# Padded pitches for the stationary operands, and a first input projection issued term by term

## What is computed

```python
def reference(...):
    x = first_block(x, ...)    # rmsnorm, w_in (2048x4096), Fourier mixing and dilated attention,
                               # w_out, rmsnorm, w_up (2048x8192), relu^2, w_down, rmsnorm
    return second_block(x, ...)  # modulated rmsnorm, w_in_2, gated linear attention and convolution,
                                 # w_out_2, SwiGLU with 5632 hidden columns, rmsnorm
```

```python
proj = jnp.einsum('bsd,de->bse', u, w_in[layer])     # the first input projection
...
a = jnp.square(jax.nn.relu(jnp.einsum('bsd,df->bsf', u, w_up[layer])))
h = h + jnp.einsum('bsf,fd->bsd', a, w_down[layer])
...
x_next = x_next + gt2 * ((silu(h2 @ w_ffn_gate) * (h2 @ w_ffn_up)) @ w_ffn_down)
```

## Time and profile before

| | us |
|---|---|
| median of 3 runs | 2323.5 (2321.68 to 2323.79) |
| the profiled execution, its own time | 2323.11 |
| its span, first to last instruction | 2321.4 |
| mean granted TensorE clock | 0.996 of full speed |

### The profile page before, as it was taken

How to read it: one execution, slowest core, us unless ns; L and a number is a source line. 1 busy time by engine, 2 the same in 40 slices (tenths; PEclk the granted TensorE clock), 3 DMA queues, 4 the chain that set the end, 5 groups by cost and what they waited for, 6 DMA issues and landing times.

```text
span 2321.4 us, 29200 instructions
## 1 busy us (share of the span) xinstructions
PE 2281.5 (98%) x10465; PEld 1878.2 (81%) x10465; DVE 1539.1 (66%) x1822; ACT 1108.7 (48%) x1515; POOL 146.2 (6%) x213
## 2 busy tenths in 40 slices
PE   8999999999999999999999999998999999999997
PEld 6888888888878888888878877787888888888886
DVE  7987658868867877886767665556545544555545
ACT  5445455545544545545563463544444344444444
POOL 1110001101111111110001000000000000000000
PEclk9999999999999999999999999999999999999999
DMA  9884459888887898886677663564555655555553
GB/s 342 294 277 154 146 180 319 305 277 289 280 290 248 270 304 263 276 278 214 219 239 249 210 202 127 196 211 156 189 192 184 216 188 193 188 193 195 186 181 109
DMA packets 245188, 523.92 MB, mean 226 GB/s; under 512 B 20016, under 2 KB 20288, under 8 KB 243776
## 3 DMA queue, kind: packets, MB, share of 16 engines
q1 hardware_dynamic: 213680, 404.80, 53.4%
q0 software_dynamic: 29568, 111.97, 13.9%
q10 hardware_dynamic: 1808, 5.37, 0.6%
HBM read 517.87 MB, written 4.21 MB: 225 GB/s over the span
## 4 chain that ended last, share of the span: by engine, by line
PE 94%; DVE 3%; issue 1%; ACT 1%; DMA 0%; ACTq 0%; DVEq 0%; POOLq 0%
PE acc L1595 29%; PE acc L1597 29%; PE acc L1596 29%; PE tp L1610 2%; DVE wlo L957 1%; PE m L1621 1%; DVE macc L977 1%; PE tp L1919 0%; ACT whi L493 0%; PE tp L1937 0%; PE tp L1931 0%; PE tp L1844 0%; PE m L1729 0%; PE tp L1905 0%; DMA mring<-w_mod 0%
## 5 line engine op out<-in xcount | busy, mean ns | idle before, releaser
L493 ACT ACTIVATE whi<-wring 128x1024 fp32r<-128x1024 f32 x776 | 812.8, 1051 | 1067.7 <-PE acc L1597 1064.5
L957 DVE TENSOR_TENSOR wlo<-wring,whi 128x1024 fp32r<-128x1024 f32 x776 | 932.6, 1213 | 581.6 <-ACT whi L493 577.7
L1595 PE MATMUL acc<-whi,xhi 128*128 128x512 f32 x2112 | 831.8, 394 | 1.8 <-DVE wlo L957 1.6
L1597 PE MATMUL acc<-whi,xlo 128*128 128x512 f32 x2112 | 822.8, 390 | 0.0
L1596 PE MATMUL acc<-wlo,xhi 128*128 128x512 f32 x2112 | 822.3, 389 | 0.0
L1595 PEld LDWEIGHTS acc<-whi,xhi 128*128 128x128 f32 x2112 | 396.8, 188 | 92.8 <-issue 11.8
L1597 PEld LDWEIGHTS acc<-whi,xlo 128*128 128x128 f32 x2112 | 396.6, 188 | 83.4
L1596 PEld LDWEIGHTS acc<-wlo,xhi 128*128 128x128 f32 x2112 | 396.9, 188 | 80.8 <-issue 0.7
L977 DVE SCALAR_TENSOR_TENSOR macc<-mring,csil,macc 128x512 f32<-128x512 f32 x480 | 344.2, 747 | 36.3 <-DMA mring<-w_mod 30.1
L1597 PE MATMUL acc<-whi,alo 128*128 128x512 f32 x608 | 238.0, 391 | 3.6 <-issue 3.6
L1595 PE MATMUL acc<-whi,ahi 128*128 128x512 f32 x608 | 240.1, 395 | 1.3 <-DVE wlo L957 1.2
(11 more groups left out here) (226 smaller groups left out, 1050.4 us busy)
## 6 DMA issues: line engine op xcount, KB each, us to landing
wring<-w_up SPq DMA_DIRECT2D x216, 512.0 KB, 4.6
wring<-w_down SPq DMA_DIRECT2D x216, 512.0 KB, 5.0
mring<-w_mod POOLq DMA_DIRECT2D x192, 512.0 KB, 5.2
wring<-w_in SPq DMA_DIRECT2D x184, 512.0 KB, 5.5
wring<-w_gate SPq DMA_DIRECT2D x88, 512.0 KB, 4.4
wring<-w_out SPq DMA_DIRECT2D x64, 512.0 KB, 4.8
gbig<-ctx_in POOLq DMA_DIRECT2D x2, 1024.0 KB, 9.3
hspill<-h ACTq DMA_DIRECT2D x1, 2048.0 KB, 7.9
```

The source lines that it names most:

```text
L493: act.activation(whi[:, piece_slot(c, piece), 0:half], wring[:, g4, piece * half:(piece + 1) * half], ACT.Copy).then_inc(hi_done, 1)
L957: dve.tensor_tensor(wlo[:, h4, 0:half], wring[:, g4, piece * half:(piece + 1) * half], whi[:, h4, 0:half].bitcast(F32), ALU.subtract).then ...
L1595: pe.matmul(dst, hi[:, tile, rows], whi[:, h4, w], start=(kg == first and k == 0), stop=False)
L1597: last = pe.matmul(dst, lo[:, tile, rows], whi[:, h4, w], start=False, stop=(kg == final and k == KG - 1))
```

## The change

Three things are changed. `xhi` and `xlo` are declared with 260 values for each k tile, of which 256 are used: a pitch of 1040 bytes. `ahi` and `alo` get 258 (1032 bytes), `bhi` and `blo` 257 (1028 bytes). To make room, `vrows` shares its place with `blk`, which is written later; an unused tensor `fill` keeps `gbig` on the place of `ctx_place`. The second change is in `multiply`: with `by_term=True` the 6 matmuls of a k tile are issued as hi·whi for t = 0 and 1, hi·wlo for t = 0 and 1, lo·whi for t = 0 and 1. This is used in blocks 1 to 7 of the first input projection. Each PSUM bank receives the same three products in the same order.

```diff
-        xhi = sb("xhi", [P, KT, S], F32R)
-        xlo = sb("xlo", [P, KT, S], F32R)
+        xhi = sb("xhi", [P, KT, S + 4], F32R)[:, :, 0:S]
+        xlo = sb("xlo", [P, KT, S + 4], F32R)[:, :, 0:S]
...
-        vrows = sb("vrows", [P, 3, P])
...
+        with ExitStack() as ph:
+            vrows = sb("vrows", [P, 3, P], scope=ph)
         blk = sb("blk", [P, T, NB])
...
-            ahi = sb("ahi", [P, KT, S], F32R, scope=ph)
-            alo = sb("alo", [P, KT, S], F32R, scope=ph)
+            ahi = sb("ahi", [P, KT, S + 2], F32R, scope=ph)[:, :, 0:S]
+            alo = sb("alo", [P, KT, S + 2], F32R, scope=ph)[:, :, 0:S]
...
+            sb("fill", [P, 4 * KT], scope=ph)
             gbig = sb("gbig", [P, 2 * D], scope=ph)
...
-            bhi = sb("bhi", [P, KT, S], F32R, scope=ph)
-            blo = sb("blo", [P, KT, S], F32R, scope=ph)
+            bhi = sb("bhi", [P, KT, S + 1], F32R, scope=ph)[:, :, 0:S]
+            blo = sb("blo", [P, KT, S + 1], F32R, scope=ph)[:, :, 0:S]
...
-            def multiply(hi, lo, kgs, kgroups, pair, order=None, operand=None):
+            def multiply(hi, lo, kgs, kgroups, pair, order=None, operand=None, by_term=False):
...
-                            for t in range(T):
+                            for term, (x, w_part) in enumerate(((hi, whi), (hi, wlo), (lo, whi)) if by_term else ()):
+                                for t in range(T):
+                                    last = pe.matmul(acc[:, 2 * pair + t, :], x[:, tile, t * P:(t + 1) * P], w_part[:, h4, w],
+                                                     start=(kg == first and k == 0 and term == 0),
+                                                     stop=(kg == final and k == KG - 1 and term == 2))
+                            for t in range(0 if by_term else T):
...
-                    multiply(xhi, xlo, range(3), 4, n % 2)
+                    multiply(xhi, xlo, range(3), 4, n % 2, by_term=True)
                     if n % 2 == 0:
                         reduce_mod(32, True)
-                    multiply(xhi, xlo, (3,), 4, n % 2)
+                    multiply(xhi, xlo, (3,), 4, n % 2, by_term=True)
```

## The result

The changed kernel takes 2362.8 us (median of 3 runs, 2362.67 to 2362.84) against 2323.5 us before: a ratio of 1.0173, with a 95% interval of 1.0154 to 1.0191. That is 39.3 us more, outside the range of 2262 to 2346 us, on the side that had the smallest chance. The profiled execution took 2362.7 us, with a span of 2361.0 us, 39.6 more than before.

What follows compares the result with a forecast made beforehand. The prediction took TensorE's rate of 226.7 ns per matmul as the bound. Its terms summed 0 + 0 + 0 against the profiled 2323.1 us and the median of 2323.5, giving 2323.3 us, with a range of 2262 to 2346.

Steps and rivals of the forecast that it cites:

- What bounds the kernel: Whole kernel: TensorE's rate, 9216 matmuls at 226.7 ns, 2089 of 2321.4 us; one nanosecond of the rate is 9.2 us.
- Part 1, can it quicken the stream: Pitches of the stationary operands in `multiply`: no quicker stream, taken as 0, with −99 us as the end.
- The second reading: Projections, w_up and w_ffn_down: distances 0, 512, 256 and 768 modulo 1024 bytes all have 226.7 ns; counted against a gain.
- Part 1, can it slow the loads: Weight loads in `multiply`: misaligned starts stay hidden behind the stream, taken as 0; other end 23 us more.
- rival C: Loads starting off 16 bytes need more than 226.7 ns and TensorE waits: 2346 to 2380 us; chance 0.14.
- A: Rival: the matmul stream quickens through starts finer than 128 bytes; at most −99 us, 2224, half of it 2274; chance 0.2.
- the bound of 99 us: Largest gain in `multiply`: all 9216 matmuls at the 216 ns of plain float32, 10.7 ns less each.
- The writes: Some 150 ScalarE and VectorE instructions writing rows with a small hole: 0 per instruction; `vrows` and `fill` also 0.
- Part 2, term by term: New order of 672 matmuls in the first projection's blocks 1 to 7: 0, with ends −7.2 and +2.2 us.
- Rival B: Gap in w_up and lower clock after idling are spared, together 7.0 us, giving 2316; chance 0.07 with the term order's −7.2.

## Why the prediction was wrong

**What bounds the kernel** was right. TensorE is the path in both, the producers stayed behind their cover, and one nanosecond of the rate was worth what the prediction said: the 5 to 6 ns found in the settled rows are the 39 us.

**Part 1, can it quicken the stream:** no gain was right, but the reason given is the step that failed, for it also ruled out a loss. The prediction took 113.3 ns for 256 columns with a load of 32 and 226.7 for 512 with a load of 128 for one law, 17/16 of the columns, and concluded that the loss goes with the columns streamed and so can't depend on the stationary's place. Two things differed between those rows, the columns and the load, and two points can't tell them apart. With full loads 256 columns take 120.0 ns. The loss is about the same for each matmul, 13.3 to 15 ns with a full load, and 6.7 ns in `multiply_rank`. That this part belongs to a meeting of load and stream is argued and not shown. What is shown is that the place of the stationary operand changes the rate: 226.7 ns at distance 0, 228.9 to 234.3 at nearly all others, for the worse and never for the better. The term that the prediction put at 0 was 39 us.

**The second reading was blind.** Distances of 0, 256, 512 and 768 with one rate were taken as evidence that the distance doesn't matter. All four are the same modulo 256. In `multiply_rank` the distance does change, between 0 and 128 modulo 256 from one k tile to the next (a weight slice there has 128 bytes), and the rate stays; but its loads have 32 columns. The prediction saw part of this ("no row shows a distance that isn't" a multiple of 128) and gave the unseen side a chance of 0.2 for a gain, but for a loss only by another mechanism.

**Part 1, can it slow the loads:** rival C had the sign and nearly the time, 2346 to 2380, by the wrong mechanism. The loads didn't grow: the group of x still means 188 ns, as the page of after has it.

```profile
L1602 PEld LDWEIGHTS acc<-whi,xhi 128*128 128x128 f32 x1888 | 355.1, 188 | 89.5 <-issue 9.8
```

And starts off 16 bytes were not the condition: x, whose starts all are multiples of 16, has 30 of the 47 us in the sum above. C priced 1704 matmuls at 13.3 ns; in fact nearly all 9216 lost something, 5 to 6 ns in the mean of a stage. The bound of the cost was therefore set by one candidate's mechanism (a longer load hidden behind 226.7 ns), and not by the nearest row of a disturbed stream, which the prediction had in hand and used for part 2 only: 230 ns after transposes. That 3.3 ns on 9216 matmuls is 30 us, 2354; with it the range would have reached most of the way. Its own test half worked: "Part 1 is wrong if the distance differs between x, a and b, in the order of 16, 8 and 4 bytes". The distance from start to start does differ, but in another order (231.6, 233.3, 232.6), which fits neither A nor C. Two smaller slips change nothing here: the range begins at 2262 although A's half, which it was to end with, is 2274, and the bound of 99 us takes 256 columns of plain float32 for 512 steps of the array, which no row shows.

The Trainium skill, in "TensorE: Matmul & The Clock Gate", section "Part 2: What happens when you issue a matmul", was cited for the claim that loading takes no bandwidth from a running matmul. The trace disagrees in effect: with loads and streams of the same size and length, 226.7 became 233.3 ns by the place of the stationary operand alone. The measurement decides; what hinders what there, no run shows.

**The writes**, `vrows` and `fill`: nothing, as predicted. ScalarE's busy time went from 1108.7 to 1109.2 us and VectorE's from 1539.1 to 1540.4.

**Part 2, term by term:** zero, as predicted, and shown alone (1.0003). In the changed kernel 12 starts of the first projection, in the new order, take as long as in the old order at the same k tile.

**Rival B**, the gap in w_up, happened in a small way on the other side of the account. TensorE's timeline of the changed kernel there:

```profile
705.14 0.40 PE L1603 MATMUL acc<-wlo,ahi 128*128 128x512 f32 x1
708.84 0.40 PE L1604 MATMUL acc<-whi,alo 128*128 128x512 f32 x1 [3.30 <-issue]
...
709.53 0.45 PE L1604 MATMUL acc<-whi,alo 128*128 128x512 f32 x1
709.78 0.63 PE L1602 MATMUL acc<-whi,ahi 128*128 128x512 f32 x1
...
713.18 0.41 PE L1604 MATMUL acc<-whi,alo 128*128 128x512 f32 x1
```

The gap is 3.70 us where it was 3.95. After it the matmuls ran at the lower clock, 1.2 GHz, for about 3.5 us, where before it was 5.2 us, from the end of the gap to the end of the stretch of the earlier trace rows. Half of that is lost time, so the two together gave back 0.25 + 0.85 = 1.1 us. The wait of this kind in w_up was between 1.6 and 3.3 us in the experiments, so a difference of one or two microseconds between single runs says little.

## What to carry to other kernels

Before the place or the pitch of a matmul's operand is changed, work out the distance between streamed and stationary starts modulo 256 bytes, and keep it; with full loads of 128 columns and float32r streams of 512 a distance of 0 was the quickest found, 240 cost 0.4%, and every other one tried cost 1 to 3.4% of the rate. Equal rates at several places are evidence only for places that differ modulo the period which might matter. A law from two rows (here "17/16") holds only if one thing differs between them; where it carries the forecast, the nearest disturbed row should bound the loss.

## What the runs showed of the hardware

- A float32r matmul of 128 by 128 stationary columns and N streamed ones, in a settled row, took N/2.4 ns + 13.3 to 15 ns at distance 0 (N = 256: 120.0, N = 384: 175, N = 512: 226.7). At the 18 other distances tried N = 512 took 227.6 to 234.3 in the mean, and 233.3, which is + 20.0, at seven of them. With a stationary of 32 columns N = 256 took 113.3, + 6.7; there too the mean rose by 3 ns, from 113.6 to 116.6, in the changed kernel. These are means: at distance 0 nearly every settled interval is within 2 ns of 226.7, at 248 within 1 ns of 233.3, and at the other places single intervals lie between 225 and 242 ns.
- Moving both operands by 128 bytes left x at 226.7 ns; moving one of them made 232.4 to 233.3 ns. In `multiply_rank` distances of 0 and 128 in turn both went with 113.3 ns.
- The rate is in part a state of the row and not of the single matmul: at distance 252 stretches of some 250 matmuls ran at 226.7 ns and the others at 233.3.
- Loads of fewer columns at distance 0 made a stream of 512 columns slower (229.8 to 231.7 ns for x). Loads of 96 columns that begin at distance 128 and end where the full ones did had 227.1.
- Open: what it is in SBUF or the array that has this period of 256 bytes, why 240 is nearly as good as 0 while 248 and 252 are not, how neighbouring matmuls influence each other, and whether a load is in step by its end.
